# A decoder trunk: the third projection chunk's queries projected transposed, their rotary step done on features by tokens

## The reference

```python
proj = h @ w_in          # qa, ka, va, qb, kb, vb, qi, ki, wi
qa = rope(heads(qa, 8), pos); ka = rope(heads(ka, 2), pos)     # sliding-window group, with sinks
qb, kb = rope(...), rope(...); qi, ki = rope(...), rope(...)   # sparse group and its indexer
ya = swa_with_sinks(qa, ka, va, sinks)
yb = dsa_sparse_attention(qb, kb, vb, qi, ki, wi)
y = concat([rms_norm(ya, g_a), rms_norm(yb, g_b)]) @ w_o

def rope(x, pos):        # x1, x2: the two halves of each 64 features of a head
    return concat([x1 * cos - x2 * sin, x2 * cos + x1 * sin])
```

## Time and profile before

| what | us |
|---|---|
| median of 3 runs | 1247.16 (1245.42 to 1247.32) |
| the profiled execution | 1246.32 |
| its span, first to last instruction | 1244.6 |
| PE busy | 1208.8 |
| DVE busy | 946.6 |
| ACT busy | 593.8 |
| POOL busy | 357.1 |
| mean granted TensorE clock | 0.997 of full speed |

### The profile page before, as it was taken

How to read it: one execution, slowest core, us unless ns; L and a number is a source line. 1 busy time by engine, 2 the same in 40 slices (tenths; PEclk the granted TensorE clock), 3 DMA queues, 4 the chain that set the end, 5 groups by cost and what they waited for, 6 DMA issues and landing times. The chain is left out here.

```text
span 1244.6 us, 20806 instructions
## 1 busy us (share of the span) xinstructions
PE 1208.8 (97%) x7370; PEld 1057.7 (85%) x7370; DVE 946.6 (76%) x1634; ACT 593.8 (48%) x1206; POOL 357.1 (29%) x341
## 2 busy tenths in 40 slices
PE   5999999999999999999999999999999999999997
PEld 5787886889888888999888688778989998899986
DVE  6899987767788795776876599858796776377648
ACT  3655668345333233555245466871545552255520
POOL 4247226610121001221117367581012200122200
PEclk9999999999999999999999999999999999999999
DMA  9873002334888422334823220114223333133331
GB/s 357 322 250 106 18 3 68 131 123 133 269 280 279 155 84 86 103 106 148 305 87 117 68 68 2 34 52 170 85 73 101 115 118 105 59 115 112 116 108 68
DMA packets 44876, 158.65 MB, mean 127 GB/s; under 512 B 5872, under 2 KB 5872, under 8 KB 44784
## 3 DMA queue, kind: packets, MB, share of 16 engines
q1 hardware_dynamic: 30528, 109.07, 26.8%
q0 software_dynamic: 12960, 47.19, 11.1%
q10 hardware_dynamic: 1296, 1.17, 0.3%
HBM read 155.31 MB, written 2.10 MB: 126 GB/s over the span
## 5 line engine op out<-in xcount | busy, mean ns | idle before, releaser
L1623 ACT ACTIVATE w_hi<-w_raw 128x1024 fp32r<-128x1024 f32 x104 | 108.4, 1060 | 152.5 <-PE bank L835 140.2
L833 PE MATMUL bank<-w_hi,hT_hi 128*128 128x512 f32 (+2 forms) x392 | 147.9, 377 | 3.0 <-ACT pq L1661 2.0
L2084 DVE TENSOR_TENSOR w_lo<-w_raw,w_hi 128x1024 fp32r<-128x1024 f32 x96 | 123.6, 1302 | 29.3 <-ACT w_hi L1623 27.9
L835 PE MATMUL bank<-w_hi,hT_lo 128*128 128x512 f32 (+2 forms) x392 | 142.6, 364 | 0.0
L834 PE MATMUL bank<-w_lo,hT_hi 128*128 128x512 f32 (+2 forms) x392 | 142.3, 363 | 0.0
L708 POOL TENSOR_TENSOR w_raw<-ada_w,w_raw 128x512 f32<-128x512 f32 x28 | 37.1, 1324 | 363.6 <-DVE w_lo L2638 201.0
L1305 PE MATMUL bank<-hT_lo,w_hi 128*128 128x256 f32 x448 | 112.3, 283 | 0.0
L1303 PE MATMUL bank<-hT_hi,w_hi 128*128 128x256 f32 x448 | 112.3, 283 | 0.0
L833 PE MATMUL bank<-w_hi,gu_hi 128*128 128x512 f32 x264 | 102.9, 390 | 0.0
L835 PE MATMUL bank<-w_hi,gu_lo 128*128 128x512 f32 x264 | 102.7, 389 | 0.0
L834 PE MATMUL bank<-w_lo,gu_hi 128*128 128x512 f32 x264 | 102.7, 389 | 0.0
(11 more groups left out here) (305 smaller groups left out, 3266.7 us busy)
## 6 DMA issues: line engine op xcount, KB each, us to landing
w_raw<-in_weights SPq DMA_DIRECT2D x184, 512.0 KB, 3.6
ada_w<-in_w_ada POOLq DMA_DIRECT2D x76, 512.0 KB, 5.3
ada_w<-in_w_ada SPq DMA_DIRECT2D x4, 512.0 KB, 6.6
qT<-in_w_ada SPq DMA_DIRECT2D x4, 512.0 KB, 10.1
xs<-in_x SPq DMA_DIRECT2D x4, 512.0 KB, 15.5
g_row<-in_ln_row POOLq DMA_DIRECT2D x4, 512.0 KB, 6.3
b_row<-in_ln_row POOLq DMA_DIRECT2D x4, 512.0 KB, 7.1
trunk_out<-xs SPq DMA_DIRECT2D x8, 256.0 KB, 2.0
```

Source lines behind the costliest of these rows:

```text
L833: pe.matmul(dst, a_hi, b_hi, start=first, stop=False)
L835: return pe.matmul(dst, a_lo, b_hi, start=False, stop=last)
L1623: nc.scalar.activation(w_hi[:, p % RING, :], w_raw[:, p % RING, :], ACT.Copy).then_inc(hi_ready, 1)
L2084: nc.vector.tensor_tensor(w_lo[:, p % RING, :], w_raw[:, p % RING, :], w_hi[:, p % RING, :].bitcast(F32), ALU.subtract).then_inc(lo_ready, 1)
```

## The change

The queries of chunk 2 are projected with the weights as the stationary operand (128 columns) and hT as the moving one (512 tokens), so that block b of 128 features (two heads) stands in PSUM with features on partitions. ACT evacuates it to pq as before. Then four transfers issued by ACT copy its 32-partition quarters to scratch (b = 0, 1) or gt_row (b = 2, 3) with neighbours exchanged, and POOL multiplies the exchanged copy by a sine table, pq by a cosine table and writes the sum straight to qT. transpose_q and copy_q are gone for chunk 2. The tables in this layout (wide) are made once, in layer 0: DVE copies cos_t and sin_t twice each into pT, PE transposes 8 blocks, ACT copies two banks. PE's first index scores wait for them, since their banks are reused. The scores of the first unit wait for POOL's sum (roped) of their block, and DVE's mask step for the same. The SBUF kept for descriptors of POOL's transfers is set to 8192 bytes.

```diff
         def at_chunk(l, c, t):
-            return 20 * l + 4 * c + t + 1
+            return 16 * l + 4 * (0, 1, None, 2, 3)[c] + t + 1
...
+        def at_swap(l, c):
+
+            return 64 * (l + 1)
+
+        def swap_part(c, b):
+
+            row = gt_row if b >= 2 else scratch
+            return row[:, b % 2 * SEQ:(b % 2 + 1) * SEQ]
...
+            def rope_queries(l, c, b):
+
+                v, w = pq[:, (c // 2) % 2, b, :], swap_part(c, b)
+                if (l, c, b) == (0, 2, 0):
+                    pool.wait_ge(wide_ready, 2)
+                pool.wait_ge(swapped[b], at_swap(l, c))
+                nc.gpsimd.tensor_tensor(w, w, wide[:, 1, :], ALU.mult)
+                nc.gpsimd.tensor_tensor(v, v, wide[:, 0, :], ALU.mult).then_inc(rotated, 1)
+                pool.wait_ge(rotated, at_roped(l, c, b))
+                if l > 0:
+                    pool.wait_ge(scored, 64 * l)
+                nc.gpsimd.tensor_tensor(qT[:, (c // 2) % 2, b, :], v, w, ALU.add).then_inc(roped, 1)
...
                 for t in range(T):
-                    rope(l, 2, t)
+                    rope_queries(l, 2, t)
+                pool.wait_ge(roped, at_roped(l, 2, T - 1))
                 for t in range(T):
                     rope_keys(l, t)
...
+            def query_block(dst, l, c, j, b):
+
+                p = PHASES[c][0] + j
+                s = slot(l, p)
+
+                def columns(w, kk):
+                    at = kk * CW[c] + b * P
+                    return w[:, s, at:at + P]
+
+                if b == 0:
+                    pe.wait_ge(hi_ready, converted(l, p))
+                for kk in range(CK[c]):
+                    k = j * CK[c] + kk
+                    pe.matmul(dst, columns(w_hi, kk), hT_hi[:, k, :], start=k == 0, stop=False)
+                    pe.matmul(dst, columns(w_hi, kk), hT_lo[:, k, :], start=False, stop=False)
+                if b == 0:
+                    pe.wait_ge(lo_ready, converted(l, p))
+                for kk in range(CK[c]):
+                    k = j * CK[c] + kk
+                    m = pe.matmul(dst, columns(w_lo, kk), hT_hi[:, k, :], start=False, stop=k == KD - 1)
...
+            def transpose_tables():
+
+                pe.wait_ge(qk_ready, at_chunk(0, 0, T - 1))
+                pe.wait_ge(tables_doubled, 1)
+                for table in range(2):
+                    for t in range(T):
+                        cols = slice(t * P, (t + 1) * P)
+                        m = pe.transpose(bank[6 + table][:, cols], pT[:, table, cols], ident[:])
+                m.then_inc(tables_transposed, 1)
...
+                    if n == 0:
+                        pe.wait_ge(wide_ready, 2)
...
+                if u == 0:
+                    pe.wait_ge(roped, at_roped(l, 2, h // 2))
...
-                project(l, 2, 0, 1)
+                project_queries(l, 0)
                 for t in range(T):
                     transpose_q(l, 0, t)
-                project(l, 2, 1, 2)
+                project_queries(l, 1)
+                if l == 0:
+                    transpose_tables()
                 for t in range(T):
                     transpose_keys(l, 1, t)
...
-                for t in range(T):
-                    transpose_q(l, 2, t)
+                pe.wait_ge(idx_acc, 24 * (l + 1))
...
+            def swap_halves(l, c, b):
+
+                act.wait_ge(proj_evac, at_evac(l, c, b))
+                if b < 2:
+                    act.wait_ge(roped, at_roped(l, 0, T - 1))
+                else:
+                    act.wait_ge(keys_roped, at_roped(l, 1, T - 1))
+                for q in range(4):
+                    to, of = (slice(n * HD // 2, (n + 1) * HD // 2) for n in (q, q ^ 1))
+                    act.dma_start(swap_part(c, b)[to, :], pq[of, (c // 2) % 2, b, :]).then_inc(swapped[b], 16)
...
                 convert(l, C0P[3] + 1)
+                if l == 0:
+                    act.wait_ge(tables_transposed, 1)
+                    for table in range(2):
+                        nc.scalar.activation(wide[:, table, :], bank[6 + table][:], ACT.Copy).then_inc(wide_ready, 1)
                 copy_keys(l, 1)
...
                         evacuate(l, 2, n - 1)
+                        swap_halves(l, 2, n - 1)
                 convert(l, C0P[4] + 3)
...
-                for t in range(T):
-                    copy_q(l, 2, t)
...
-                    dve.wait_ge(qk_transposed, at_chunk(l, 2, T - 1))
+                    dve.wait_ge(roped, at_roped(l, 2, n))
...
+            def double_tables():
+
+                for n, table in enumerate((cos_t, sin_t)):
+                    for half in range(2):
+                        m = nc.vector.tensor_copy(pT[:, n, :].rearrange("p (t two d) -> p t two d", t=T, two=2)
+                                                  [:, :, half, :], table[:])
+                m.then_inc(tables_doubled, 1)
...
                     for t in range(2, T):
                         rope_direct(t)
+                    double_tables()
                     convert(l, C0P[1] + 3)
...
-    nc = bacc.Bacc("TRN2", target_bir_lowering=False, num_devices=1)
+    nc = bacc.Bacc("TRN2", target_bir_lowering=False, num_devices=1, dynamic_dma_scratch_size=8192)
```

More of the change, by code:

```diff
@@ L197, in build_trunk @@
         exp_first = sb("exp_first", [P, 1])
+        wide = sb("wide", [P, 2, SEQ])
         sb("ahead_of_shared", [P, 24])
@@ L347, in build_trunk @@
         rope_table = sem("rope_table")
+        tables_doubled = sem("tables_doubled")
+        tables_transposed = sem("tables_transposed")
+        wide_ready = sem("wide_ready")
+        swapped = [sem(f"swapped{i}") for i in range(4)]
         t_raw = sem("t_raw")
@@ L441, in at_chunk @@
         def at_chunk(l, c, t):
-            return 20 * l + 4 * c + t + 1
+            return 16 * l + 4 * (0, 1, None, 2, 3)[c] + t + 1
         def at_evac(l, c, t):
-            return at_chunk(l, c, t) - T
+            return 20 * l + 4 * c + t + 1 - T
+        def at_swap(l, c):
[3 more added lines that the diff above has]
+            return row[:, b % 2 * SEQ:(b % 2 + 1) * SEQ]
         def at_roped(l, c, t):
@@ L463, in qk_bank @@
         def qk_bank(c, t):
-            return {0: 4 + t, 2: (4, 6, 7, 4)[t], 4: 2}[c]
+            return {0: 4 + t, 4: 2}[c]
         def index_bank(h):
@@ L1020, in project_first, with project_queries @@
                             transpose_x(2 * l, T - 1, 4)
+            def query_block(dst, l, c, j, b):
[15 more added lines that the diff above has]
+                    m = pe.matmul(dst, columns(w_lo, kk), hT_hi[:, k, :], start=False, stop=k == KD - 1)
+                if b == T - 1:
+                    m.then_inc(piece_used, 1)
+                elif j == CP[c] - 1:
+                    m.then_inc(tile_done, 1)
+            def project_queries(l, j):
+                for b in range(T):
+                    if j == 0:
+                        if l == 0:
+                            pe.wait_ge(rotated, at_roped(l, 0, b))
+                        else:
+                            pe.wait_ge(proj_evac, at_evac(l, 0, b))
+                    query_block(bank[BANKS[2] + b][:], l, 2, j, b)
+            def transpose_tables():
[6 more added lines that the diff above has]
+                m.then_inc(tables_transposed, 1)
             def project(l, c, j0, j1):
@@ L1035, in project, with finish_queries @@
                 accumulate(l, c, j0, j1, hT_hi, hT_lo, CK[c], CW[c], wait_tile)
[L1037 to L1053, removed]
+            def finish_queries(l, b):
+                for j in range(2, PHASES[2][1]):
+                    query_block(bank[BANKS[2] + b][:], l, 2, j, b)
             def project_keys(l, j, tiles):
@@ L1091, in transpose_q @@
                     pe.wait_ge(proj_evac, at_evac(l, 1, t))
[L1092 to L1095, removed]
                 else:
```

## The result

The changed kernel takes 1252.99 us (median of 6 runs, 1251.24 to 1255.43) and the kernel before 1245.78 (6 runs, 1245.42 to 1247.32): a ratio of 1.0056, 95% interval 1.0045 to 1.0067. It is slower by 7.2 us, stands 4.4 us above the predicted 1248.6, and 1 us beyond the upper end of the range. (The three runs that the prediction started from had a median of 1247.16; six have 1245.78. As a change, 7.2 us were measured and 1.5 forecast.) The profiled execution of the changed kernel is the slowest of its six, 1255.43 us with a span of 1253.8.

The account below looks back on a forecast made before the run. The prediction took TensorE (PE), busy for 97% of the span, as the bound. Its terms +1.1 +1.1 -0.7 + 0 = +1.5 us, on the median 1247.16, gave 1248.6 us, range 1246.0 to 1252.0.

Parts of the forecast that it names:

- Part 1: Chunk 2's query projection on PE: as many matmuls, 96 a layer, at the same price with operands swapped; cost 0.
- Part 2: Removed query transposes and ACT copies: POOL's last key tile limits PE, so only 0.7 us is gained over both layers.
- The rival by which the transposes count in full: POOL does not limit the key transposes, PE's 1.78 us per layer comes through: -1.4, 1245.8 us; chance 0.11.
- Parts 3 and 4: Making the tables in layer 0: DVE's four copies +1.1 us, PE's table transposes and ACT's two copies +1.1 us.
- Hidden they were not: Rival: DVE makes up the time of its table copies before 73.11, so they are hidden: +0.4, 1247.6 us; chance 0.10.
- Part 5: Exchange transfers on ACT's queue and POOL's turn: covered by 1.1 us before POOL is wanted for the keys; cost 0.
- the four signs of being wrong: No PE wait for POOL; POOL's first key operation over 0.3 us later; clock under 1; a relu waiting for the issues.
- The point from which POOL late decides: Three issue intervals and a landing over about 4.0 us, against 2.9 forecast: POOL's last sum then meets DVE's conversions.
- POOL late: Rival: transfers and issues on ACT delay POOL, one key collision more in both layers: +4.6, 1251.8 us; chance 0.19.
- the clock rival: PE's idle time before the last key transpose drops the clock, 1.7 us a fall: 1250.3 us for one; chance 0.12.

Follow-up runs that it names:

- e9: The changed kernel without the exchange transfers (POOL multiplies unexchanged queries) and with tables filled by a constant: 1244.99 us, ratio to before 0.9997.
- e3b: The kernel before without chunk 2's query transposes and their copies, nothing put in: 1245.19 us, ratio to before 0.9995.
- e1: The changed kernel without the 32 transfers; POOL multiplies the unexchanged queries by the sine table: 1246.95 us, ratio to before 1.0012.
- e6: The changed kernel with each block's four transfers issued half by SP and half by ACT: 1248.85 us, ratio to before 1.0028.
- e2: The changed kernel with five unread 128x256 matmuls filling PE's waits for the turned keys, in both layers: 1251.18 us, ratio to before 1.0040.
- e12: The changed kernel with all transfers issued by SP between its weight loads, none by ACT: 1251.80 us, ratio to before 1.0048.
- e11: The changed kernel with ACT's four issues a block moving 2 KB constants to an unread tile, POOL multiplying unexchanged queries: 1249.88 us, ratio to before 1.0030.
- e4: The changed kernel without the making of the wide tables, which POOL fills with a constant: 1252.93 us, ratio to before 1.0056.
- e10: The changed kernel with only two of each block's four transfers, the lower two quarters: 1246.85 us, ratio to before 1.0010.

## Why the prediction was wrong, point by point

- **Part 1, the projection itself: 0.** Right; e9 has the new form and its intervals are those of e3b, which has the old one (43.64 and 43.61 against 43.68).
- **Part 2, the transposes: -0.7.** Right, in size and in reason: e3b shows -0.35 a layer, and PE's 1.78 becomes a wait for POOL. The rival by which the transposes count in full is refuted by it.
- **Parts 3 and 4, the tables: +2.2.** The mechanism was right and the terms together 0.4 us too large. Together they measured 1.72 to 1.78 us: DVE's copies 0.81 (65.02 to 65.83) where I had taken 1.1, PE's and ACT's share the other 0.9 to 1.0, where I had taken 1.1. Hidden they were not.
- **Part 5, the transfers and POOL's turn: 0.** This is the step that failed. Without it the sum +1.5 stands: e1, which has all but the transfers, measured 1.0012, 1.5 us. The last query sum was to end 28.9 us behind kiT (116.3 - 87.38) and ended at 31.0 (120.93 - 89.92), when the keys had been there for 0.95 us. The issue is 0.61 us instead of 0.34 to 0.37; I had taken the price from one issue on this queue, which moves 512 KB to 128 partitions, and named 0.6 only for the question whether four fit ahead of a relu. The trace of the kernel before has seven more at its start, of 0.42 to 0.66 us, two of them here:

```profile
2.77 0.61 ACTq L1974 DMA_DIRECT2D lnc<-in_ln_col  x1
3.94 0.66 ACTq L1975 DMA_DIRECT2D nsink<-in_sinks  x1
```

And I had held the issues against the widest gap alone, 2.42 us, which lies behind the last evacuation. The three gaps ahead of it were 2.09, 2.30 and 2.17 us and have become 2.60, 2.52 and 2.52: relu, evacuations, index sums and DVE's conversions all move back, the last evacuation from 21.38 to 22.41 us behind kiT. The landing is 2.0 us by the median (I took 1.8), at most 3.4 for layer 0's first block and 3.5 for layer 1's second. The last block was to be ready 3.0 us behind its evacuation and was ready 4.0 behind (112.96 to 116.95), itself 1.0 us later. That a late first block is made good by the third did not hold in e6, where POOL's chain behind it had no idle time. Of the four signs of being wrong that the prediction lists, three came: the late key operation, the clock, the relu behind the issues.
- **The point from which POOL late decides** (three intervals and a landing over about 4.0 us) was put too high: 3 x 0.61 + 2.0 = 3.8 lies under it, and POOL was late all the same. It took the last evacuation as fixed, which the issues carry back by 1.0 us, and DVE's conversions as standing still at 116.12: they start 1.2 us later behind kiT (29.91 instead of 28.74) and, with POOL busy beside them, last 4.98 us instead of 3.75. So they reach over one more of POOL's key operations. Before had two such collisions, so this was the third, and its price 0.87. The last query sum itself took 1.29 us beside the conversions, against 1.30 before, and did not suffer.
- **The rivals were not alternatives.** POOL late (+4.6) and the clock (+1.7 a fall) had chances and prices of their own, 1251.8 and 1250.3, and the result is both: POOL's lateness makes PE wait 2.8 us ahead of the key transposes, and behind this wait the clock is at half. Of the 7.2 us, by medians: 1.5 are the forecast's terms (e1 beside its own runs of before, 1245.48), 4.2 POOL's lateness with the clock kept (e2 beside e1) and 1.8 the clock (the changed kernel beside e2, whose runs overlap, so that this size is rough); that they add up to 7.5 is the 0.3 by which the two medians of before differ. The idle time that I put into the clock rival, 1.4 us a layer, did not lower it (e1 and e3b stay at 1.00), and a fall costs 1.26 to 1.45 us here by the profiles, not 1.7.

The Trainium skill, "TensorE: Matmul & The Clock Gate", part 1, has activity lift the clock and its lack lower it; the windows after agree: clock 0.50 behind stretches with PE busy for 0.68 and 0.52 us of 2, and 1.00 in e2 where the same stretch is filled.

Open: in which executions the clock falls. It fell in both layers of the changed kernel's and e12's profiled executions, in layer 0 only of e11's and in layer 1 only of e4's, with nearly the same waits: e4's are 0.35, 1.22 and 1.22 us in layer 0, where the clock stayed at 1.00, and 0.35, 1.21 and 1.22 in layer 1. How much of POOL's lateness each cause makes in the changed kernel itself, the issues that carry the evacuations back or the landings, is not split either; e11 and e6 show only that each can bring a third collision. A way to exchange the halves with two transfers, which e10 says would cost nothing, was not tried, nor was e6 or e12 with the clock kept.

## What to carry to other kernels

A new transfer costs its issuing engine time too: price the issue from a transfer of its own shape, or from both ends, and ask what is queued behind it on that engine. When a chain is late at a meeting point, the engines that it meets may be carried along or not: work out where both stand, not only the one that is late. And if a rival's mechanism makes an engine idle, take the clock into that rival's price instead of giving it a chance of its own.

## What the runs showed of the hardware

- An issue of a 64 KB transfer between SBUF tensors, 32 partitions each, took 0.61 us on ACT's queue and 0.59 on SP's (e12) by the median, against 0.34 us for a 512 KB transfer. The longest of the changed kernel's 32 took 1.94 us, and where ACT and SP issued side by side (e6), ACT's took 0.69 to 0.74. The size in bytes did not matter (e11: 2.44 us for four of 2 KB).
- The same 128x128 operation on POOL takes 0.46 us alone and 1.3 to 1.44 beside DVE's 128x1024 subtraction. DVE can pay too: three of these subtractions take 3.75 us in e1, and 4.98 where POOL works beside them with hardly a gap (after, e6, e12).
- The start of an execution is not fixed: ACT's 128x1024 piece starts at 62.6 to 64.4 us of the span in these thirteen executions, whatever the kernel. That is 1.8 us of the scatter of single times, and it is over before the changed part begins.
